# A two-layer decoder step on one core: v's transposes, top-k rounds and page numbers at other places, q.k pairs first in a round, and the bias table turned by a row pitch

## What is computed

```python
def select_topk(scores, q_pos, k_pos, topk):
    admissible = k_pos[None, None, :] <= q_pos[None, :, None]
    _, idx = lax.top_k(jnp.where(admissible, scores, -jnp.inf), topk)
...
    logits = jnp.einsum('bqkgd,bqjkd->bqkgj', qg, k_sel).astype(jnp.float32) * HEAD_DIM ** -0.5
    bias = rel_bias[t5_bucket(q_pos[None, :, None] - sel_pos)].astype(jnp.float32)
...
    logits = jnp.where(valid[:, :, None, None, :], logits + bias, -jnp.inf)
    p = jax.nn.softmax(logits, axis=-1).astype(v_sel.dtype)
    out = jnp.einsum('bqkgj,bqjkd->bqkgd', p, v_sel)
```

## Time and profile before

| | us |
|---|---|
| median of three runs (1347.73 to 1349.34) | 1349.33 |
| the profiled execution itself | 1351.15 |
| its span | 1349.4 |
| TensorE busy (PE matmul) | 1256.8 (93%) |
| VectorE busy | 702.3 (52%) |
| ScalarE busy | 470.2 (35%) |
| GpSimd busy | 193.0 (14%) |
| mean granted clock of TensorE | 0.963 |

### The profile page before, as it was taken

The page is one execution under the profiler, slowest core; times in us unless marked ns, Lnnn a source line. Parts: engine busy times, 40 slices in busy tenths (PEclk is TensorE's granted clock), DMA queues, the critical chain, the costliest instruction groups (busy, mean ns, idle before and its releaser), DMA issues.

```text
span 1349.4 us, 24444 instructions
## 1 busy us (share of the span) xinstructions
PE 1256.8 (93%) x9991; PEld 1213.2 (90%) x9993; DVE 702.3 (52%) x1279; ACT 470.2 (35%) x548; POOL 193.0 (14%) x285
## 2 busy tenths in 40 slices
PE   5998994795999999999999999999999999999995
PEld 5878993563899999999999999999899999999994
DVE  5267786767347555555522244644755555552323
ACT  5243235451224434343322234332543343432110
POOL 0111001106303111111100010030411111110000
PEclk9999997696799999999999999999999999999998
DMA  7143301002222222222222332112122222222211
GB/s 271 64 149 123 132 33 46 1 2 65 68 93 70 89 91 93 93 93 93 87 89 109 102 125 94 64 64 93 63 94 93 93 93 93 93 86 87 86 60 63
DMA packets 25992, 118.17 MB, mean 88 GB/s; under 512 B 7720, under 2 KB 9192, under 8 KB 13904
## 3 DMA queue, kind: packets, MB, share of 16 engines
q1 hardware_dynamic: 21184, 105.50, 22.4%
q0 software_dynamic: 2048, 10.54, 2.3%
q10 hardware_dynamic: 2704, 1.35, 0.4%
HBM read 113.91 MB, written 3.46 MB: 87 GB/s over the span
## 4 chain that ended last, share of the span: by engine, by line
PE 70%; DVE 2%; POOL 1%; ACT 1%; issue 0%; DVEq 0%
PE ps L814 22%; PE ps L815 22%; PE ps L817 22%; POOL xl L1802 1%; PE ps L831 1%; PE ps L950 1%; PE ps L947 1%; PE ps L948 1%; PE ps L1209 0%; DVE acc L1240 0%; DVE vtc L1765 0%; DVE yt L1794 0%; PE ps L1121 0%; DVE rstd L1244 0%; DVE xn L1244 0%
## 5 line engine op out<-in xcount | busy, mean ns | idle before, releaser
L814 PE MATMUL ps<-xh,w_h 128*128 128x260 f32 x1792 | 471.4, 284 | 7.9 <-POOL xl L1802 7.8
L815 PE MATMUL ps<-xl,w_h 128*128 128x260 f32 x1792 | 469.6, 283 | 0.0
L817 PE MATMUL ps<-xh,w_l 128*128 128x260 f32 x1792 | 361.0, 283 | 0.0
L814 PEld LDWEIGHTS ps<-xh,w_h 128*128 128x128 f32 x1792 | 339.4, 189 | 9.1 <-issue 7.6
L815 PEld LDWEIGHTS ps<-xl,w_h 128*128 128x128 f32 x1792 | 338.8, 189 | 0.1
L1233 DVE TENSOR_TENSOR w_l<-w_raw,w_h 128x2048 fp32r<-128x2048 f32 (+1 forms) x94 | 211.6, 2251 | 166.4 <-ACT w_h L503 166.2
L817 PEld LDWEIGHTS ps<-xh,w_l 128*128 128x128 f32 x1792 | 277.1, 189 | 0.0
L815 PE MATMUL ps<-hl,w_h 128*128 128x260 f32 x704 | 183.9, 282 | 0.0
L503 ACT ACTIVATE w_h<-w_raw 128x2048 fp32r<-128x2048 f32 (+1 forms) x50 | 92.3, 1846 | 262.2 <-PE ps L817 242.4
L814 PE MATMUL ps<-hh,w_h 128*128 128x260 f32 x704 | 183.4, 282 | 0.0
L947 PE MATMUL ps<-xh,w_h 128*128 128x260 f32 x448 | 128.9, 309 | 14.1 <-DVE xl L1253 12.5
(11 more groups left out here) (298 smaller groups left out, 1406.3 us busy)
## 6 DMA issues: line engine op xcount, KB each, us to landing
w_raw<-in_wstream SPq DMA_DIRECT2D x86, 1024.0 KB, 4.8
w_raw<-in_wstream SPq DMA_DIRECT2D x8, 768.0 KB, 4.2
res<-in_x_t SPq DMA_DIRECT2D x4, 520.0 KB, 8.3
out_y<-yt SPq DMA_DIRECT2D x8, 260.0 KB, 2.2
tabf<-bias_by_distance SPq DMA_DIRECT2D x1, 2048.0 KB
wm<-in_sgu_w ACTq DMA_DIRECT2D x1, 512.0 KB, 3.6
sb_b<-in_sgu_b ACTq DMA_DIRECT2D x1, 512.0 KB, 4.2
out_f<-ost SPq DMA_DIRECT2D x2, 198.0 KB, 4.6
```

Of the source, the lines that this page charges most:

```text
L814: pe.matmul(out[h], wh, hi[h], start=(first and k == 0), stop=False)
L815: pe.matmul(out[h], wh, lo[h], start=False, stop=False)
L817: ins = pe.matmul(out[h], wl, hi[h], start=False, stop=(last and k == nk - 1))
```

## The change

1. **v.** The four transposes of v go into slab 9, behind its step 12 (`turn_values`), into PSUM bank 4; VectorE copies them to `vn` ahead of `evac_b(9)`.
2. **Top-k and page numbers.** The table of rounds holds all 48; the first half of the page numbers is computed behind `evac_b(6)`, the second (`page_terms_out`) stays behind slab 9. GpSimd no longer waits for the gate products.
3. **q.k pairs.** `p_work` issues `p_pair` of the next round first.
4. **Bias table.** SyncE writes each of the eight rows of `fneg` 128 times to DRAM, behind load 3. Behind load 5 it reads the table with a pitch of 639 elements from copy to copy, so that each partition starts one element earlier: the rows arrive turned. `flip`, `tabf`, the eight `table` products and ScalarE's eight copies go, and load 2 no longer stands behind the wait for `f_ev`. VectorE waits for the table at the first logits. GpSimd begins without its wait.

```diff
-        flip = at("flip", [P, P], F32, o_gg + 5120)
-        tabf = at("tabf", [P, 8, SEQ], F32, o_ik)
...
-        scratch = nc.dram_tensor("bias_by_distance", (8, 640), F32)
+        scratch = nc.dram_tensor("bias_by_distance", (8, P, 640), F32)
...
-            sp.wait_ge(f_ev, 2)
-            sp.dma_start(scratch.ap(), fneg[:]).then_inc(d_scr, 16)
             for s in range(2, 10):
                 sp.wait_ge(w_hi, s - 1)
                 sp.wait_ge(w_lo, s - 1)
                 load(s, s % 2)
-                if s == 2:
+                if s == 3:
+                    sp.wait_ge(f_ev, 2)
+                    sp.dma_start(scratch.ap(), fneg[:].rearrange("p (a c) -> p a c", a=1).broadcast_to((8, P, 640)))\
+                        .then_inc(d_scr, 16)
+                if s == 5:
                     sp.wait_ge(d_scr, 16)
-                    sp.dma_start(tabf[:], bass.AP(scratch.ap().tensor, 0, [[1, P], [640, 8], [1, SEQ]])).then_inc(d_scr, 16)
+                    for h in range(2):
+                        sp.dma_start(tab[:].rearrange("p (j h) c -> p h j c", h=2)[:, h],
+                                     bass.AP(scratch.ap().tensor, 4 * h * P * 640 + P - 1,
+                                             [[639, P], [P * 640, 4], [1, SEQ]])).then_inc(d_tabs, 16)
...
-                if g in (1, 2) and step % 4 == 3:
-                    table(4 * (g - 1) + step // 4)
...
+                if g == 9 and step == 12:
+                    turn_values()
+
+            def turn_values():
+
+                pe.wait_ge(ev_a, NUNITS_I - 1)
+                for n in range(NCH):
+                    ins = pe.transpose(ps[:, 4, n * P:(n + 1) * P], vt[:, n * P:(n + 1) * P], ident[:])
+                ins.then_inc(vn_tr, 1)
...
             def p_work(rnd):
 
+                for i in heads(rnd + 1):
+                    if i % 2 == 0:
+                        p_pair(i // 2)
                 for i in heads(rnd - 1):
                     p_turn(i)
...
-                for i in heads(rnd + 1):
-                    if i % 2 == 0:
-                        p_pair(i // 2)
...
-            rounds = {4: (0, 0, 3), 5: (4, 4, 2), 6: (4, 4, 2), 7: (4, 4, 2), 8: (0, 0, 0), 9: (4, 5, 0)}
+            rounds = {4: (0, 0, 4), 5: (4, 6, 2), 6: (4, 5, 2), 7: (4, 6, 3), 8: (0, 0, 1), 9: (4, 3, 0)}
...
+                if g == 9:
+                    dve.wait_ge(vn_tr, 1)
+                    dve.wait_ge(d_kvi, 48)
+                    dve.tensor_copy(vn[:].rearrange("p n c -> p (n c)"), ps[:, 4, :]).then_inc(vn_ev, 1)
                 evac_b(g)
+                if g == 6:
+                    page_columns()
...
-            dve.wait_ge(vn_tr, 1)
-            dve.wait_ge(d_kvi, 48)
-            dve.tensor_copy(vn[:].rearrange("p n c -> p (n c)"), ps[:, 2, :]).then_inc(vn_ev, 1)
-            page_columns()
-            topk_rounds(q, 3 * ROUNDS - q)
+            page_terms_out()
...
+                if i == 0:
+                    dve.wait_ge(d_tabs, 32)
                 dve.wait_ge(qk_done, i + 1)
...
-            pool.wait_ge(tab_ev, 8)
...
-            pool.wait_ge(gate_mm, 8)
```

More of the change, by code:

```diff
@@ L88, in build_step @@
     (wstream, x_t, vec, rg_w, h0, conv0, ffn0, pages, page2, cache_kv, cache_i, rel, rel4, sgu_w, sgu_b,
-     sgu_w0, sgu_b0, c_ident, c_flip, c_dist, c_blocks, c_pick, c_slots) = ins
+     sgu_w0, sgu_b0, c_ident, c_dist, c_blocks, c_pick, c_slots) = ins
     y_o, k_o, v_o, ki_o, h_o, c_o, cv_o, f_o = outs
@@ L292, in build_step @@
         d_st, hst_done, ap_mm = sem("d_st"), sem("hst_done"), sem("ap_mm")
-        d_flip = sem("d_flip")
+        d_tabs = sem("bias_table")
         d_wax, d_rgs, d_pt = sem("d_wax"), sem("d_rgs"), sem("d_pt")
@@ L298, in build_step @@
         setup_v = sem("setup_v")
-        f_mm, f_ev, tab_mm, tab_ev = sem("f_mm"), sem("f_ev"), sem("tab_mm"), sem("tab_ev")
+        f_mm, f_ev = sem("f_mm"), sem("f_ev")
         wi_tr, wi_nat, idx_mm, relu_done, score_acc, causal, topk_done = (
@@ L414, in _ @@
             load(1, 1)
-            for dst, src, done in ((flip, c_flip, d_flip), (pt, pages, d_pt), (pg2, page2, d_const),
+            for dst, src, done in ((pt, pages, d_pt), (pg2, page2, d_const),
                                    (blocks, c_blocks, d_const), (picks, c_pick, d_const), (h0s, h0, d_rgs)):
                 sp.dma_start(dst[:], src).then_inc(done, 16)
-            sp.wait_ge(f_ev, 2)
-            sp.dma_start(scratch.ap(), fneg[:]).then_inc(d_scr, 16)
             for s in range(2, 10):
@@ L541, in gelu_of @@
                 act.activation(gg[:, 2 * g - 15, :], gg[:, 2 * g - 15, :], ACT.Gelu_apprx_tanh).then_inc(gelu_b, 1)
-            def table(m):
-                act.wait_ge(tab_mm, m + 1)
-                act.activation(tab[:, m, :], ps[:, 4 + m % 2, :], ACT.Copy).then_inc(tab_ev, 1)
             def relu(i):
@@ L839, in bias_products @@
                 pe.matmul(ps[0:8, 5, 0:128], relt[:], dist[:, 512:640], start=True, stop=True).then_inc(f_mm, 1)
[L841 to L847, removed]
             def turn_weights():
-                pe.wait_ge(tab_ev, 8)
                 pe.wait_ge(d_c, 16)
@@ L974, in _ @@
                 ins.then_inc(gate_mm, 1)
-            for n in range(NCH):
-                ins = pe.transpose(ps[:, 2, n * P:(n + 1) * P], vt[:, n * P:(n + 1) * P], ident[:])
-            ins.then_inc(vn_tr, 1)
             pe.wait_ge(sig_done, 8)
@@ L1398, in page_columns, with page_terms_out @@
                 ch.link(ts(pgc[:, 1, :], pgf[:, 1, :], float(P), None, ALU.mult))
+            def page_terms_out():
                 dve.tensor_copy(ptab[:, NK:NK + 1], col("chunk", 0))
@@ L1456, in _ @@
             ch.link(dve.memset(quart1, 16384.0))
-            dve.wait_ge(vn_tr, 1)
-            dve.wait_ge(d_kvi, 48)
-            dve.tensor_copy(vn[:].rearrange("p n c -> p (n c)"), ps[:, 2, :]).then_inc(vn_ev, 1)
-            page_columns()
-            topk_rounds(q, 3 * ROUNDS - q)
+            page_terms_out()
+            assert q == 3 * ROUNDS
             dve.wait_ge(pstep, 2)
@@ L1950, in shape_constants @@
                             2.0 * P * (p % 16)], 1).astype(np.float32)
-    return ident, np.ascontiguousarray(ident[::-1]), dist, blocks, picks, slots, np.concatenate([mod4, extra], 1)
+    return ident, dist, blocks, picks, slots, np.concatenate([mod4, extra], 1)
 def kernel(**a):
@@ L1988 @@
     cols = lambda t: t.reshape(-1, P).T
-    ident, flip, dist, blocks, picks, slots, columns = shape_constants()
+    ident, dist, blocks, picks, slots, columns = shape_constants()
     rel4 = np.zeros((P, P), np.float32)
@@ L2014 @@
         "sgu_b0": np.repeat(a["sgu_b"][0, :, 0][None], P, axis=0),
-        "c_ident": ident, "c_flip": flip, "c_dist": dist, "c_blocks": blocks, "c_pick": picks, "c_slots": slots,
+        "c_ident": ident, "c_dist": dist, "c_blocks": blocks, "c_pick": picks, "c_slots": slots,
     }
```

2 lines of the change are left out of this document (removed).

## The result

| | before | changed |
|---|---|---|
| median (lowest to highest), us | 1348.53 (1346.38 to 1349.34) | 1369.82 (1365.54 to 1370.79) |
| span of the profiled execution | 1349.4 | 1368.1 |
| mean granted clock of TensorE | 0.963 | 0.945 |

The changed kernel takes 1.0154 times as long, 95% interval 1.0129 to 1.0179: 1.5% slower, some 21 us. The forecast was slower by 6 us, and the time lies 8.8 us above the end of the range.

The account below looks back on a forecast made before the run. TensorE's matmuls in the slabs and VectorE's list between 209 and 240 were taken to hold the path. Terms of -22.2, +26.7 (stall) and +1.5 (clock) made +6.0 us, median 1355.3 us, range 1324 to 1361.

Parts of the forecast that it names:

- The write: SyncE's 2.62 MB bias-table write at 51 GB/s ends at 81.5, delays load 4; TensorE stalls 26.7 us for `win`.
- The rivals of a hidden or half hidden write: Hidden: write under 25 us, no stall, 1327 us, chance 0.30; half hidden: 25 to 42 us, 1328-1346 us, chance 0.10.
- the likeliest case: The forecast itself: write of 45 to 56 us, median 1355.3 us, own range 1348 to 1361 us, chance 0.52.
- TensorE's table products: Slabs 1 and 2: eight `table` products of 0.86 us each leave TensorE, -6.9 us.
- Behind slab 9: VectorE's list there shrinks, ScalarE becomes the limit, `rg_share` begins near 225.4 instead of 240.17: -14.8 us.
- q.k pairs: Pairs first in a round: -1.5 us, about 0.3 us in each of eight two-round periods; bounds -4 and +1.
- The round in slab 4: Four top-k rounds instead of three ahead of the `ikt` copy TensorE waits for; nothing hides it: +1.0 us.
- at slab 9: TensorE waits 1.8 us at its start, v's transposes add 0.5, copy-out saves 0.7: gate products begin 1.6 us later.
- The clock at large: TensorE's half clock after the long stall for `win` in slab 3: 1.5 us added.
- The third rival: Added rounds delay copy-outs at TensorE's starts of slabs 5 and 9: gain 6.2 us less, 1361.5 or 1333 us, chance 0.08.

Follow-up runs that it names:

- c_rounds: `c_last` with another table of top-k rounds (three instead of four in slab 4, two instead of three last in slab 7): 1326.79 us, ratio 0.9827.
- a_pairs_last: The changed kernel with the q.k pairs last in `p_work` again: 1361.25 us, ratio 1.0068 to the kernel before.
- b_pitch: The kernel before with part 4 of the change alone (bias table read with a pitch of 639): 1373.1 us, ratio 1.0161.
- c_last: The changed kernel with the bias table's copies made from DRAM to DRAM and the q.k pairs last in a round: 1332.01 us, ratio 0.988.
- c_warm: `c_last` with 15 unused filling matmuls where TensorE waits behind slab 9: 1332.16 us, ratio 0.9869 to the kernel before.

## Why the prediction was wrong

- **The write, right.** 51 GB/s (the forecast's row), landed at 80 (81.5), a wait of 25.2 us (26.7); the table's path alone 21.7 us (21.3). The rivals of a hidden or half hidden write fell. It rested on one row of 0.2 us, and the chances leaned the other way (0.47 for faster, 0.39 for slower): that the sign came out as in the likeliest case is in part luck.
- **TensorE's table products, right**: -5.9 us for seven of them, -6.0 counted.
- **Behind slab 9, right**: -16.4 us, with ScalarE's exponential as the new limit; `rg_share` follows the copy-out by 15.0 us.
- **q.k pairs, wrong in sign: the first failing step.** The prediction says "it is the order of a full queue that changes, and the sum of a round stays", takes -1.5 us and bounds it by -4 and +1. The order costs 7.8 us alone by the medians and 5.9 us in the rounds of each pair of traces, past the bound. I read TensorE's busy share in a window of the rounds with one head and let it speak for those with two, which aren't in that window. There VectorE and ScalarE pass two buffers round, which what is put ahead of the turns delays (1.3 us), and the half clock then lasts some 13 us longer, and the rest arises under both. A busy share doesn't show it anyway: TensorE was busy 12.85 of 13 us in the slowed stretch and did fewer matmuls.
- **The round in slab 4, the second failing step, a term too small: +1.0 us for the wait, +4.2 measured** (with slab 5; 2.9 on average over the profiles with and without that round). "Nothing hides it" was right, and 4.8 us of waiting came as forecast; but the price of a wait is the wait and the half clock behind it. The rows for that stood in the prediction, used for the long stall and not here. The same holds at slab 9: 1.3 us of waiting (1.8 forecast), +2.9 us with v's transposes (+1.6).
- **The clock at large: 1.5 us counted** for the one long stall. By the mean granted clocks what was withheld of full speed rose from 0.037 x 1349.4 = 50 us to 0.055 x 1368.1 = 75 us. Some 14 of the 25 us more lie in slab 3 (0.57 granted from 60 to 92 us, 1.00 before), nearly all of it idle, where it costs nothing; 3.5 in slab 5, 1.7 in slab 9, and some 8 behind the bisection (0.55 granted from 316 to 380 us; before, 0.62 from 306 to 360), where the time grew by 2.0. From the gate products to the return of the clock in the rounds it is at half no longer than before; more of that time lies under the heads.
- **The third rival had the place right** (TensorE's starts of slabs 5 and 9) and gave it 0.08; its price of 6.2 us for the moved rounds is near the 7 us that `c_rounds` won back, mostly by the clock and not by their length.

By their ratios the parts alone make +21.7 (table), -12.3 (v, top-k, page numbers) and +7.8 (pairs), 17.2 us; the change as a whole makes +20.8. The first two together are additive (9.4 against 9.2 of `a_pairs_last`). The 3.6 us left are within the intervals, which are 2.4 to 3.7 us to either side for each of the four ratios.

## What to carry to other kernels

A DMA that replicates eight partitions 128 times ran at 51 GB/s, the rate of a single small write from them: write the small piece once and replicate it inside DRAM, and put no load behind it in its queue. Before moving something ahead in a full queue, look for what stands behind it and hands back a buffer; a busy share taken where the buffers aren't short says nothing of where they are, and a queue that is busy throughout can still do less. And price each new wait of TensorE with the stretch at half clock that followed the last such wait: here two top-k rounds of 2.5 us together, moved two slabs on, were worth 7 us by the medians (some 4 to either side), and the version with all three mended (DRAM copies, pairs last, `c_rounds`' table) is 1.7% faster than the kernel before and 3.2% faster than the changed one.

## What the runs showed of the chip that I had not expected

- The write from eight source partitions was slow twice over: the DMA engines were busy 0.47 of the time at 51 GB/s and 1.05 at 420 GB/s. Never more than nine packets were in flight, against sixteen and more, and each took nearly four times as long (0.38 against 0.10 us).
- Loads in another queue pass such a write; they are slowed (13.2 us to landing instead of 4.8), not stopped.
- After a wait of 3.9 us the clock was at half for 3.4 us (before) or for 10 x 0.34 / 0.5 = 6.8 us (`b_pitch`, 126 to 136 us). After 4.8 to 4.9 us it was at half for 10 us (the changed kernel), 13.7 us (`c_last`) or 9 x 0.38 / 0.5 = 6.8 us (`c_warm`, 98 to 107), and slab 5 took 28.8, 29.2 and 26.3 us. The clock isn't the same from run to run, and a prediction can only give it a range.
